# Two transformer blocks on one core: weighted x into the MLP, a later convolution, a shorter last expert round, turned tables, and one rounded product for the head norms

## The reference

```
h = rms_norm(x, norm_mix);  x = x + (gates * branches).sum() @ w_out
h = rms_norm(x, norm_ffn);  x = x + conv_ffn(h, w_gate, w_up, conv_w, conv_b, w_down)   # 2816 wide
```

```
mod = silu(c) @ w_ada + b_ada                      # six vectors
h = x * (1 + scale1) + shift1
q, k: rms norm per head and rotation; o_a = attention
u, v = gelu(z);  v = layer_norm(v);  o_b = u * (w_s @ v + b_s)     # 8 tables of 128 x 128, within 128 tokens
y = (sigmoid(gate_a) * (o_a @ w_a) + sigmoid(gate_b) * (o_b @ w_b)) @ w_out
x = layer_norm(ALPHA * x + gate1 * y);  h = x * (1 + scale2) + shift2
scores = sigmoid(h @ router_w)                     # 64 experts, top 8 in 4 of 8 groups
y = sum over the chosen experts of weight * (silu(h @ w_gate) * (h @ w_up)) @ w_down, and a shared expert
x = layer_norm(ALPHA * x + gate2 * y)
```

## Time and profile before

| | us |
|---|---|
| runs | 3566.52, 3567.25, 3570.82; median 3567.25 |
| profiled execution, its own time | 3552.64 |
| its span | 3550.8 |
| TensorE busy | 3179.1 (90%) |
| VectorE busy | 1601.0 (45%) |
| ScalarE busy | 983.4 (28%) |
| GpSimd busy | 218.1 (6%) |
| mean granted TensorE clock | 0.946 of full |
| moved by DMA | 752.36 MB, mean 212 GB/s |

### The profile page before, as it was taken

How to read it: one execution, slowest core, us unless ns; L and a number is a source line. 1 busy time by engine, 2 the same in 40 slices (tenths; PEclk the granted TensorE clock), 3 DMA queues, 4 the chain that set the end, 5 groups by cost and what they waited for, 6 DMA issues and landing times. The chain is left out here.

```text
span 3550.8 us, 46373 instructions
## 1 busy us (share of the span) xinstructions
PE 3179.1 (90%) x14440; PEld 2039.6 (57%) x14441; DVE 1601.0 (45%) x4106; ACT 983.4 (28%) x2061; POOL 218.1 (6%) x212
## 2 busy tenths in 40 slices
PE   7888999979999898988998999779899799998995
PEld 5555668758777657774444444366587544444444
DVE  2565466656565364443233233264634532323235
ACT  4464352323232343330111111132532211111111
POOL 0000000000000000000111111100000011111111
PEclk9898999989999999988999999989999799999997
DMA  5202126734543302316999999671031399999985
GB/s 205 73 2 72 27 86 186 223 108 147 185 137 125 129 19 60 101 57 246 405 404 408 401 390 409 274 285 40 16 98 52 147 393 409 393 402 402 387 347 225
DMA packets 287451, 752.36 MB, mean 212 GB/s; under 512 B 25743, under 2 KB 167265, under 8 KB 230984
## 3 DMA queue, kind: packets, MB, share of 16 engines
q1 hardware_dynamic: 234312, 632.62, 46.8%
q0 software_dynamic: 27648, 67.51, 4.8%
q10 hardware_dynamic: 25344, 50.33, 4.2%
HBM read 724.85 MB, written 58.72 MB: 221 GB/s over the span
## 5 line engine op out<-in xcount | busy, mean ns | idle before, releaser
L2751 PE MATMUL up_ps<-experts,x_turned 128*64 128x512 f32 (+1 forms) x2256 | 697.9, 623 | 98.2 <-DMA experts<-in_w_up_dram 80.5
L2751 PEld LDWEIGHTS up_ps<-experts,x_turned 128*64 128x64 f32 (+1 forms) x2256 | 269.8, 160 | 454.7 <-issue 447.3
L289 DVE TENSOR_TENSOR pieces_lo<-weights,pieces_hi 128x512 fp32r<-128x512 f32 (+1 forms) x468 | 316.0, 684 | 460.0 <-ACT pieces_hi L283 459.3
L283 ACT CAST pieces_hi<-weights 128x512 fp32r<-128x512 f32 (+1 forms) x468 | 284.3, 614 | 574.6 <-PE gate_ps L301 164.2
L2775 PE MATMUL y_ps<-experts,hid_turned 128*64 128x512 f32 (+1 forms) x1128 | 345.6, 601 | 1.6 <-ACT hid_turned L2831 1.6
L2898 DVE TENSOR_TENSOR hid_seats<-up_ps,gated 128x256 f32<-128x256 f32 x94 | 57.5, 612 | 579.1 <-ACT gated L2824 579.1
L299 PE MATMUL gate_ps<-h_hi,pieces_hi 128*128 128x512 f32 x624 | 249.3, 400 | 32.0 <-DVE pieces_lo L289 32.0
L2824 ACT ACTIVATE gated<-up_ps 128x256 f32<-128x256 f32 x94 | 36.1, 384 | 774.0 <-PE up_ps L2751 774.0
L300 PE MATMUL gate_ps<-h_lo,pieces_hi 128*128 128x512 f32 x624 | 246.7, 395 | 0.0
L301 PE MATMUL gate_ps<-h_hi,pieces_lo 128*128 128x512 f32 x624 | 246.2, 395 | 0.0
L2775 PEld LDWEIGHTS y_ps<-experts,hid_turned 128*64 128x64 f32 (+1 forms) x1128 | 117.4, 154 | 222.3 <-issue 222.3
(11 more groups left out here) (444 smaller groups left out, 4999.2 us busy)
## 6 DMA issues: line engine op xcount, KB each, us to landing
experts<-in_w_gate_dram SPq DMA_DIRECT2D x141, 1024.0 KB, 10.3
experts<-in_w_up_dram SPq DMA_DIRECT2D x141, 1024.0 KB, 14.2
experts<-in_w_down_dram SPq DMA_DIRECT2D x141, 1024.0 KB, 15.8
ada_weights<-in_w_ada_dram ACTq DMA_DIRECT2D x48, 1024.0 KB, 5.2
rows_sb<-results SPq DMA_DIRECT2D x16, 2048.0 KB, 24.8
weights<-in_w_in_dram SPq DMA_DIRECT2D x57, 512.0 KB, 4.2
weights<-in_w_in_dram SPq DMA_DIRECT2D x12, 2048.0 KB, 12.3
weights<-in_w_out_dram SPq DMA_DIRECT2D x6, 2048.0 KB, 7.9
```

The lines of the kernel that those rows point to most:

```text
L283: act.copy(self.like(view, self.hi[:, i % self.BUFFERS, :, :]), view).then_inc(s["hi_ready"], 1)
L289: dve.tensor_tensor(lo, view, hi.bitcast(F32), ALU.subtract).then_inc(s["lo_ready"], 1)
L2751: made = pe.matmul(up_ps[part, b, :].rearrange("p (h n) -> p h n", h=2), xT[:, b, k, part], experts.up(b + i)[:, :, k, :], start=(k == 0), ...
```

## The change

- The constants for head norms get 52 rows: 20 sums, and the same 20 again from row 32. After the reciprocal ScalarE rounds all 52 rows, VectorE puts the rest of the rounding into rows 32 to 51, and one fp32r product over 52 rows with doubled one-hot rows spreads both at once. Scales and spreads stand one piece later. The constants are loaded in two smaller transfers, and GpSimd copies the one-hot part to fp32r.
- `norm_model` and `split_tiles` go. `residual_product` of the first block squares x, rounds x times the gain into `h_hi` and puts the rest into `h_lo`; GpSimd sums the squares of seven tiles. `conv_ffn` takes products of x without the norm, makes root and reciprocal in part 0, spreads them through a diagonal matrix, multiplies the gate half by them before the taps (`scale_gate`), and the gelu by them on GpSimd.
- In `conv_ffn` the taps, convolution and product stand later in the engines' lists.
- The gating tables and biases arrive turned and spread, and are loaded during attention; the stage for them keeps the products and the multiplications, with four banks.
- The router's weights are the stationary operand and h the moving one, 512 columns; the scores are copied and turned, then the sigmoid is taken.
- The last expert round is a step of b = 0 alone; the number of rounds is found with limits 4n + 2 and 3n + 1 in place of 4n and 3n.
- `combine` starts its banks with the first real product and not with one of zeros.

The diff, cut; SP, POOL, ACT and DVE get the same end of the round loop as PE, and `token_inputs` loads its constants as the opening does:

```diff
...
+N_ROWS = 32 + 2 * MAX_NORMED
+AT_ONES = 2 * MAX_NORMED - 2
+AT_SELECT = AT_ONES + N_ROWS
+SELECT_2 = AT_SELECT + 5 * P
+NORM_W = AT_SELECT + MAX_NORMED * P
...
-    steps = np.broadcast_to(np.concatenate([4 * np.arange(32), 3 * np.arange(32)]).astype(np.float32), (P, 64))
+    steps = np.broadcast_to(np.concatenate([4 * np.arange(32) + 2, 3 * np.arange(32) + 1]).astype(np.float32), (P, 64))
...
+    for first in (0, 32):
+        norm[np.arange(P), AT_ONES + first + side] = 1
+        for i in range(MAX_NORMED):
+            norm[first + 2 * i + side, AT_SELECT + i * P + np.arange(P)] = 1
+    return {"cst_norm": norm, "cst_lists": lists, "cst_square": square, "cst_buckets": np.concatenate(rows, axis=1), "cst_rope": rope}
...
+def gating_weights(given):
+
+    return np.ascontiguousarray(given["w_spatial_2"].transpose(0, 3, 1, 2))
+
+
+def gating_shifts(given):
+
+    b = np.repeat(given["b_spatial_2"], HD, axis=1)
+    return np.ascontiguousarray(b.reshape(LAYERS, SGU_GROUPS * HD // P, P, P).transpose(0, 2, 1, 3))
...
-            self.at_scale.setdefault(last + 3 + n // 2, []).append(n)
+            self.at_scale.setdefault(last + 4 + n // 2, []).append(n)
...
+                    at = n * P
+                    pe.matmul(spread[:, n % 2, :], prog.select[:, at:at + P], rstd[:, :], start=True,
...
+                    if i == when.at_reciprocal + 1:
+                        act.wait_ge(s["rstd_ready"], 1)
+                        act.copy(rstd[:, :], root[:, :]).then_inc(s["rstd_rounded"], 1)
...
-                        dve.reciprocal(rstd[:, :], root[:, :]).then_inc(s["rstd_ready"], 1)
+                        dve.reciprocal(root[:, :], root[:, :]).then_inc(s["rstd_ready"], 1)
+                    if i == when.at_reciprocal + 1:
+                        dve.wait_ge(s["rstd_rounded"], 1)
+                        dve.tensor_tensor(rstd[32:n_rows, :], root[32:n_rows, :], rstd[32:n_rows, :].bitcast(F32),
+                                          ALU.subtract).then_inc(s["rstd_split"], 1)
...
+                    for dst, view in loads:
+                        sp.dma_start(dst, view).then_inc(s["side_loaded"], 16)
...
-                sp.dma_start(gather[:, :], d["cst_norm"]).then_inc(s["gather_loaded"], 16)
+                sp.dma_start(gather[:, :], d["cst_norm"][:, 0:AT_SELECT]).then_inc(s["gather_loaded"], 16)
+                sp.dma_start(select[:, :], d["cst_norm"][0:N_ROWS, AT_SELECT:NORM_W]).then_inc(s["gather_loaded"], 16)
...
+                pool.tensor_copy(prog.select[:, :], select[:, :])
...
+                residual_product(prog, ring, at["w_out"], y, xT, ada=ada, x_loaded=x_loaded,
+                                 norm=(oT[:, 2, 0:3, :], norm_ffn, ffn_sums, *h))
...
-                norm_model(prog, xT, norm_ffn, hT)
-                split_tiles(prog, hT, *h)
...
+                    for m in range(1, DK - 1):
+                        pool.wait_ge(s["squared"], m + 1)
+                        if m >= 2:
+                            pool.wait_ge(s["gathered"], m - 1)
+                        pool.tensor_tensor(squares[:, 2, :], squares[:, 2, :], squares[:, m % 2, :],
+                                           ALU.add).then_inc(s["gathered"], 1)
...
+                def sum_squares(i, source):
+                    for t in range(TT):
+                        last = pe.matmul(totals[:, i, t:t + 1], source[:, t * P:(t + 1) * P], prog.ones[:, 0:1], start=True,
+                                         stop=True)
+                    last.then_inc(s["totals_ready"], 1)
...
+                def square(m):
+                    act.wait_ge(s["added"], m + 1)
+                    if m >= 3:
+                        act.wait_ge(s["gathered"], m - 2)
+                    act.activation(squares[:, m % 2 if m else 2, :], xT[:, m, :], ACT.Square).then_inc(s["squared"], 1)
+
+                def round_x(m):
+                    act.activation(h_hi[:, m, :], xT[:, m, :], ACT.Copy, scale=gain[:, m:m + 1]).then_inc(s["x_rounded"], 1)
...
+                    if norm and i % 2 == 1 and i >= 5:
+                        square((i - 5) // 2)
+                        round_x((i - 5) // 2)
...
+                def rest_of_x(m):
+                    dve.wait_ge(s["x_rounded"], m + 1)
+                    dve.scalar_tensor_tensor(out=h_lo[:, m, :], in0=xT[:, m, :], scalar=gain[:, m:m + 1],
+                                             in1=h_hi[:, m, :].bitcast(F32), op0=ALU.mult, op1=ALU.subtract)
...
+                    for m in (DK - 3, DK - 2):
+                        rest_of_x(m)
+                    dve.wait_ge(s["totals_ready"], 1)
+                    dve.tensor_copy(sums[:, 0, :], totals[:, 0, 0:TT]).then_inc(s["first_half"], 1)
+                    rest_of_x(DK - 1)
+                    dve.wait_ge(s["first_half"], 1)
+                    dve.wait_ge(s["totals_ready"], 2)
+                    dve.tensor_tensor(sums[:, 0, :], sums[:, 0, :], totals[:, 1, 0:TT], ALU.add)
...
+                    for m in range(FH):
+                        pool.wait_ge(s["gelu_ready"], m + 1)
+                        pool.tensor_tensor(taps[:, m % 2, :], taps[:, m % 2, :], spread[:, :],
+                                           ALU.mult).then_inc(s["scaled"], 1)
...
+                            if opens and m == 0 and j == 0:
+                                pe.wait_ge(s["diagonal_ready"], TT)
+                                for t in range(TT):
+                                    last = pe.matmul(spread_ps[:, t * P:(t + 1) * P], prog.ones[:, :], diagonal[:, t, :],
+                                                     start=True, stop=True)
+                                last.then_inc(s["spread_made"], 1)
...
-                        act.wait_ge(s["piece_used"], 4 * m + 2)
+                        act.wait_ge(s["gate_ready"], m + 1)
                         if m >= 2:
                             act.wait_ge(s["hid_ready"], m - 1)
-                        act.activation(taps[:, m % 2, :], gate_ps[:, m % 2, :], ACT.Copy,
+                        act.activation(taps[:, m % 2, :], gate[:, m % 2, :], ACT.Copy,
                                        scale=conv_w[:, 2, f0 + m:f0 + m + 1]).then_inc(s["tap_ready"], 1)
 
...
+                    def scale_gate(m):
+                        dve.wait_ge(s["piece_used"], 4 * m + 2)
+                        if opens and m == 0:
+                            dve.wait_ge(s["spread_ready"], 1)
+                        if m >= 2:
+                            dve.wait_ge(s["tap_ready"], m - 1)
+                            dve.wait_ge(s["conv_ready"], m - 1)
+                        dve.tensor_tensor(gate[:, m % 2, :], gate_ps[:, m % 2, :], spread[:, :],
+                                          ALU.mult).then_inc(s["gate_ready"], 1)
...
-                        dve.wait_ge(s["gelu_ready"], m + 1)
+                        dve.wait_ge(s["scaled"], m + 1)
...
+                            conv(m - 1)
                         split.rest(dve, s, 4 * m + 2)
+                        if opens and m == 0:
...
+                        scale_gate(m)
+                        if m >= 1:
+                            rest_of_hid(m - 1)
+                        ada.add_rows(dve, ADA_D)
...
-                    if 16 <= i <= 20:
-                        spread_rstd(i - 16)
-                    if i in (18, 19, 21, 23, 25):
-                        swap_pairs((18, 19, 21, 23, 25).index(i))
+                    if 17 <= i <= 21:
+                        spread_rstd(i - 17)
+                    if i in (19, 20, 22, 24, 26):
+                        swap_pairs((19, 20, 22, 24, 26).index(i))
...
-                    if 18 <= i <= 22:
-                        scale(i - 18)
-                    if i in (20, 21, 23, 25, 27):
-                        rotate((20, 21, 23, 25, 27).index(i))
+                        dve.reciprocal(root[:, :], root[:, :]).then_inc(s["rstd_ready"], 1)
+                    if i == 18:
+                        dve.wait_ge(s["rstd_rounded"], 1)
+                        dve.tensor_tensor(rstd[32:n_rows, :], root[32:n_rows, :], rstd[32:n_rows, :].bitcast(F32),
+                                          ALU.subtract).then_inc(s["rstd_split"], 1)
+                    if 19 <= i <= 23:
...
-                pe.wait_ge(s["loaded"], 48)
-                for j in range(2):
-                    for g in range(4):
-                        last = pe.transpose(turned[:, j, g * P:(g + 1) * P], w_s[:, 4 * j + g, :], prog.ident[:, :])
-                    last.then_inc(s["turned"], 1)
                 for m in range(4):
-                    last = pe.matmul(wide[:, m, :], pairs[:, m * P:(m + 1) * P], b_s[:, :], start=True, stop=True)
...
-                        last = pe.matmul(router_ps[:, t, :], hT[:, k, t * P:(t + 1) * P], rw[:, k, :], start=(k == 0),
-                                         stop=(k == DK - 1))
```

(27 more changed lines are left out.)

283 lines of the change are left out of this document (141 added, 142 removed).

## The result

The changed kernel takes 3469.23 us (median of 3 runs, 3465.12 to 3476.83) against 3567.25: ratio 0.9726, interval 0.9697 to 0.9754. A second measurement of both gave 0.9745 (0.9726 to 0.9764). Forecast were 3480.5, with 3468 to 3495 for the likeliest case. The change comes out some 11 us better than the forecast, at the lower edge of that likeliest range.

A forecast was written before the change was run, and what follows sets the result against it. TensorE, busy in 90% of the span, sets the pace in dense stages; the change works mostly on seams where it waits. The terms sum to -86.7: 3567.25 becomes 3480.5 us, range 3457 to 3512 with 0.8.

The forecast's parts named there:

- likeliest case: The summed forecast of 3480.5 us for the whole kernel, own range 3468 to 3495, chance 0.60.
- tails of mixers a, b, c: Head norms' spreads by one fp32r product, VectorE's scales setting the pace: -4.0 in mixer_a, -3.0 in mixer_b, -4.4 in mixer_c.
- token_inputs, constants with it: Quicker spreads and a shorter wait for the reciprocal, -10.0 for two layers; smaller gather constants, -0.8.
- opening: A new GpSimd copy on the stretch where VectorE normalises x: +1.0 (0 to +1.9).
- seam ahead of conv_ffn: Between residual_product and conv_ffn, 31.6 us; squares and roundings hide behind products, first product at 761.5: -22.5.
- root spread in part 0: In conv_ffn the reciprocal root enters by four f32 products between gate and up pieces: +1.3.
- tails ahead of `down`: In conv_ffn's two tails the late convolution, gelu and GpSimd product aren't hidden: +2.2 each, +4.4 (0 to +7).
- tables: Gating tables come turned, loaded during attention; `mixed` starts behind attention's last copy: -8.9 per layer, -17.8.
- router: Products gain nothing, additions cost some 1.9 per layer, the clock may rise sooner: -3.0 (bounds +3.8 and -7).
- short round: Routed experts drop the last round's second step, 94 to 92 steps: -12.4 in layer 1, -14.2 in layer 0, sum -26.6.
- zeros: In combine two 512-column products per tile go; VectorE's chain is the pace: -1.3 (0 to -4).
- The clock could rise sooner: At full clock from the start the router's loops would end 1.8 sooner in layer 0, 5.0 in layer 1.

The follow-up runs named there:

- second pair: The kernel before and the changed kernel, both unchanged, each profiled a second time: 3569.68 and 3471.19 us.
- full_round: The changed kernel with the last expert round whole again (both steps, limits 4n and 3n): 3503.83 us, ratio 0.9825 to the kernel before.
- second trace of before: The kernel before, unchanged, profiled a second time: 3569.68 us, ratio 0.9986.

## Why the prediction came out as it did

| part | forecast | by stretches of the first pair of traces, where nothing else is said |
|---|---|---|
| tails of mixers a, b, c | -11.4 | -4.7, -3.0, -4.5: -12.2 |
| token_inputs, constants with it | -10.8 | -5.2, -0.8: -6.0 (second pair -7.5) |
| opening | +1.0 | +0.8 |
| seam ahead of conv_ffn | -22.5 | -23.4; -22.2 with the products ahead of it, which ran longer at half the clock |
| root spread in part 0 | +1.3 | +0.8 |
| tails ahead of `down` | +4.4 | +2.4 |
| tables | -17.8 | -21.0 to -22.0 |
| router | -3.0 | +3.1 (means of 5 and 8 traces) |
| short round | -26.6 | -27.3 to the last scatters; -29.5 with combine, by full_round |
| zeros | -1.3 | 0 to -1 |
| sum | -86.7 | about -85 |

That the two sums agree this well is in part luck. The router and token_inputs came out 11 us worse than forecast, and the tables, the short round, the tails and the root spread 10 us better.

- **Seam, spreads, opening, the dense part**: each step held; the seam's chain was summed to 9.1 and took 8.1. The cover was TensorE, and stayed so even with GpSimd's time threefold. The rule of the Trainium skill on the shared SBUF interfaces ("GPSIMD Engine Reference", 1. Specifications) is borne out by the 0.32 us that each `pieces_lo` gained under the added load; it costs TensorE nothing in the dense part, and 2.2 in the tail.
- **Tails ahead of `down`**: mis-sized. 2.2 each were forecast, 1.2 measured; the convolution of the last tile ran while TensorE was still in its last pieces.
- **Tables**: the 8.9 per layer ahead of `mixed` measured 8.4 to 9.0 (8.1 to 8.8 against the traces of before). What was left out is some 2 per layer behind it: the 64 products with four banks, at a clock of 1.00 in place of 0.68.
- **Constants**: the size was the wrong thing to price, and the -0.8 isn't there. The wait is the queue's, 2.15 and 3.74 where 2.2 had been in both layers. Issued first, the same constants made the stage 2.3 and 5.1 shorter.
- **Short round**: up to the last scatters 29.0 were forecast and 27.3 came in the first pair of traces, 29.6 by full_round. The 1.2 per layer that the landing was to cost back isn't seen: with combine it is 29.5. (In layer 0 the forecast's own terms, 12.4 and 1.97, give 14.4 and not 14.2.)
- **Router**: the step that failed is "The clock could rise sooner", priced at 6.8 for the two loops and taken for the stage. By the means the loops became 4.4 shorter. One part of the shortfall is the price of a product at half the clock: 1.7 was taken, and 1.90 is what it took (1529.59 to 1531.49 us), against 1.60 for the eight before. The chain of copy, turning and table load, forecast at 1.9 per layer, is there in full, with 1.8. And the clock falls again behind the loop, for which the forecast had no term: 3.9 in the products behind it. The Trainium skill ("TensorE: Matmul & The Clock Gate", What's actually happening) ties the gate to how busy TensorE was; the trace agrees, with 0.50 behind the wait of 1.87, and with 0.72 and 0.62 in that stretch where the wait was filled.
- **Zeros**: TensorE was no bound on the path, as said; even the 1.3 isn't seen.

What the sum leaves open are about 10 us between 85 and the 95 to 98 of the medians. Part of them is the clock in stages whose code didn't change: the first block's merge is 2.8 shorter in eight of twelve traces with the new head norms (1.2 of it comes back in the products of residual_product, where the half clock then lies), and the attention of mixer_a averages 105 us in these twelve and 107 in the two traces of before. Another part may be the old tails: against the second trace of before, the three of the mixers gained 15.2 and not 12.2. Whether that is all of it stays open: two traces of before are too few, and each stage of this kind moves by several microseconds between executions of the same code.

## What to carry to other kernels

A seam can be priced well from its rows: list what still has to happen behind the last product, and nothing else; the seam ahead of `conv_ffn`, the two of the gating tables and layer 1's last scatter came out within 1 us. Price also what the clock does behind it: in the gating stage a shorter wait of TensorE came with some 2 us more in the products that follow, and behind a new short wait inside a stage most of what a faster loop had gained was lost again. Before a microsecond in one stage is put down to an edit, look at the clock there, and lay the window by the stage's own first product: one that reaches into the next wait shows a gap that isn't in the stage (968 to 1079 us of the kernel with GpSimd's load altered has TensorE busy for 109.84 of 111, only because the wait ahead of `down` begins at 1077.8). When a transfer is late, look at what stands ahead of it in its queue before making it smaller.

## What the runs showed of the hardware

- One and the same code ran 102.8 to 110.9 us in one stage, with a mean granted clock of 0.96 down to 0.84. The two profiles of before differ by 17 us in span with the same code, so a pair of single profiles doesn't price a change of that size.
- Behind a seam TensorE can be busy all the time at a mean clock of 0.70: 32 products in 10 us, where 44 fit at 1.00.
- GpSimd products with two SBUF operands lengthen VectorE's subtractions beside them: 0.71 us on average with GpSimd busy for 12.9 of 111 us, 1.03 with 40.6.
- Two loads of 35 and 130 KB behind 6 MB in the same queue kept TensorE waiting for 2.15 and 3.74 us; issued ahead of them, for none.
